# Operands of the matmuls placed by their byte distance modulo 256, and two AdaLN norms of the second block folded into the feed-forward that follows

## The reference, cut to what matters

```
h = modulate(rmsnorm_2(x, ffn1_norm[l]), sh1, sc1)          # norm(x) * gain * (1 + sc) + sh
x = x + 0.5 * (1 + g1) * swiglu_2(h, ffn1_w_gate[l], ffn1_w_up[l], ffn1_w_down[l])
h = modulate(rmsnorm_2(x, mix_norm[l]), sh2, sc2)
x = x + (1 + g2) * hybrid_mixer(h, ...)
h = modulate(rmsnorm_2(x, ffn2_norm[l]), sh3, sc3)
x = x + 0.5 * (1 + g3) * swiglu_2(h, ...)
return rmsnorm_2(x, final_norm)
```

## Time and profile before

| what | value |
|---|---|
| median of three runs | 2888.78 us |
| profiled execution | 2889.2 us |
| its span on the core | 2887.4 us |
| granted TensorE clock, mean | 0.982 |
| TensorE matmul busy | 2785.5 us (96%), 17408 matmuls |
| VectorE busy | 1905.4 us (66%) |
| ScalarE busy | 1200.3 us (42%) |
| GpSimd busy | 608.2 us (21%) |
| chain that ended last | TensorE 71%, VectorE 14%, issue 6%, ScalarE 4% |
| VectorE subtraction for `in_lo`, 128x2048 (336), mean | 2.40 us; 2.29 us where GpSimd is idle |
| VectorE product of 128x256 (1316, 1321) | 0.42 us |
| VectorE four splits of features (615) | 1.65 us |
| VectorE squaring 128x1024 (716) | 1.22 us |
| VectorE, two diagonals (2076) | 0.48 us |
| GpSimd, 1/rms of two columns (839, 840) | 0.19 and 0.69 us |
| a ReLU unit | 11.15 us |

### The profile page before, as it was taken

One profiled execution on the slowest core, in us unless ns is written; L12 is line 12 of the kernel. 1 busy time (PEld: TensorE's weight loads), 2 busy tenths in 40 slices (PEclk: granted clock), 3 DMA queues, 4 the chain that ended last, 5 costly groups with the idle time before them and its releaser, 6 DMA issues.

```text
span 2887.4 us, 43862 instructions
## 1 busy us (share of the span) xinstructions
PE 2785.5 (96%) x17408; PEld 2457.0 (85%) x17408; DVE 1905.4 (66%) x2046; ACT 1200.3 (42%) x1478; POOL 608.2 (21%) x510
## 2 busy tenths in 40 slices
PE   8999999999989989999899999999999989999998
PEld 8987789989878988998699898888788878888887
DVE  7885655688867885555655556666666747665665
ACT  4333444333444334334444345334433444445433
POOL 5953200068435851000100000000000320000000
PEclk9999999999999999999899999999999999999999
DMA  7755135557526764433345444545554335533542
GB/s 289 258 182 162 45 146 192 187 210 270 188 74 227 264 229 176 185 142 103 110 180 191 144 133 182 201 148 168 194 198 154 120 138 200 199 128 114 211 189 102
DMA packets 126465, 500.31 MB, mean 173 GB/s; under 512 B 11024, under 2 KB 12336, under 8 KB 92960
## 3 DMA queue, kind: packets, MB, share of 16 engines
q1 hardware_dynamic: 112768, 450.39, 42.9%
q0 software_dynamic: 13600, 48.60, 4.9%
HBM read 497.90 MB, written 1.05 MB: 173 GB/s over the span
## 4 chain that ended last, share of the span: by engine, by line
PE 71%; DVE 14%; issue 6%; ACT 4%; DMA 2%; POOL 2%; DVEq 0%; SPq 0%; ACTq 0%; POOLq 0%
PE duo L1105 7%; PE duo L1198 6%; PE duo L1202 6%; PE duo L1206 6%; PE duo L1107 5%; PE duo L1108 5%; PE duo L1115 5%; DVE down_lo L336 4%; PE duo L1114 4%; PE duo L1500 3%; PE duo L1501 3%; PE duo L1505 3%; DVE in_lo L336 3%; DVE hid_hi L1326 2%; ACT in_hi L329 2%
## 5 line engine op out<-in xcount | busy, mean ns | idle before, releaser
L336 DVE TENSOR_TENSOR in_lo<-ring_in,in_hi 128x2048 fp32r<-128x2048 f32 x296 | 709.9, 2399 | 304.7 <-ACT in_hi L329 304.5
L329 ACT CAST in_hi<-ring_in 128x2048 fp32r<-128x2048 f32 (+1 forms) x293 | 554.7, 1893 | 274.0 <-PE duo L1505 136.0
L336 DVE TENSOR_TENSOR down_lo<-ring_down,down_hi 128x1024 fp32r<-128x1024 f32 (+1 forms) x196 | 372.1, 1898 | 33.6 <-ACT down_hi L329 33.6
L1107 PE MATMUL duo<-feat,in_hi 128*128 128x256 f32 x1408 | 344.9, 284 | 4.0 <-ACT in_hi L329 3.4
L1108 PE MATMUL duo<-feat,in_hi 128*128 128x256 f32 x1408 | 343.9, 283 | 0.0
L329 ACT CAST down_hi<-ring_down 128x1024 fp32r<-128x1024 f32 (+1 forms) x196 | 260.2, 1327 | 71.4 <-PE duo L1206 70.1
L1107 PEld LDWEIGHTS duo<-feat,in_hi 128*128 128x128 f32 x1408 | 270.0, 192 | 8.7 <-ACT in_hi L329 3.8
L1108 PEld LDWEIGHTS duo<-feat,in_hi 128*128 128x128 f32 x1408 | 270.4, 192 | 3.3
L1198 PE MATMUL duo<-down_hi,hid_hi 128*128 128x512 f32 x984 | 260.0, 396 | 7.5 <-DVE hid_hi L1326 6.6
L1202 PE MATMUL duo<-down_lo,hid_hi 128*128 128x512 f32 x984 | 259.8, 396 | 0.0
L1206 PE MATMUL duo<-down_hi,hid_lo 128*128 128x512 f32 x984 | 258.7, 394 | 0.0
(11 more groups left out here) (493 smaller groups left out, 5147.5 us busy)
## 6 DMA issues: line engine op xcount, KB each, us to landing
ring_in<-in_ffn_in SPq DMA_DIRECT2D x196, 1024.0 KB, 6.2
ring_down<-in_ffn_down SPq DMA_DIRECT2D x132, 512.0 KB, 3.5
ring_down<-in_ffn_down SPq DMA_DIRECT2D x64, 1024.0 KB, 4.8
mod_w<-in_w_ada POOLq DMA_DIRECT2D x72, 512.0 KB, 5.0
ring_in<-in_sb_w_qkv SPq DMA_DIRECT2D x24, 1024.0 KB, 5.2
ring_in<-in_conv_w_in SPq DMA_DIRECT2D x12, 1024.0 KB, 5.1
ring_in<-in_gla_w_in SPq DMA_DIRECT2D x12, 1024.0 KB, 5.1
ring_in<-in_nsa_w_in SPq DMA_DIRECT2D x10, 1024.0 KB, 5.2
```

The lines of the kernel that those rows point to most:

```text
L329: act.copy(hi[:, s, 0:n], raw[:, s, 0:n]).then_inc(hi_ready.sem, 1)
L336: dve.tensor_tensor(lo[:, s, 0:n], raw[:, s, 0:n], hi[:, s, 0:n].bitcast(F32), ALU.subtract).then_inc(lo_ready.sem, 1)
L1107: pe.matmul(out, hi, self.feat_hi[:, c, :], start=opens, stop=False, skip_group_check=True)
```

## The change

Three things are done.

First, placement. `feat` gets 2 x 8 rows of 288 elements (1152 bytes) of space. Unnamed gap tiles put `in_hi` 64 bytes past the start of `feat_space` modulo 256, and `proj` and `arena` 64 bytes before `in_hi`, so that `hid_*` and `down_*` have difference 0. Two views of 256-column rows start at byte 0 of the space (`feat_near`, difference 64 to `in_hi`) and byte 64 (`feat`, difference 0). `Feed` with `for_silu` or `moves`, `RowFeed` and `FeatTurn` use `feat_near`; the others keep `feat`, and `Feed` after a `Linear` keeps `feat2`, whose difference to `in_hi` stays 64.

Second, `ShiftRowFeed` replaces `row_norm` and `pre_norm` ahead of `ffn1_in_2`, and `ShiftFeed` replaces `pre_norm` ahead of `ffn2_in_2`. They are `RowFeed` and `Feed` with the AdaLN scale as gain. `HybridOut` now transposes the first half of x between the two halves of its last unit.

Third, the offset `sh` rides along as two more feature columns: each row of features is 258 columns wide (`WIDE_FEATURE`), at a row distance of 1152 bytes, so that rows with even c have a difference of 64 to the weights and rows with odd c one of 192. Gate and up products take a PSUM bank each; VectorE copies the two columns that the offset gives (`shifts`), multiplies gate and up by 1/rms, and ScalarE adds the gate's offset inside SiLU. The pre-norm ahead of `HybridIn` stays.

```diff
-        self.feat = split("feat", 2, KC, TOKENS)
-        self.feat_hi, self.feat_lo = self.feat[:, 0], self.feat[:, 1]
+        self.feat_space = split("feat", 2 * KC * WIDE_ROW)
+        near, still = (self.feat_space[:, at:at + 2 * KC * TOKENS].rearrange("p (s c n) -> p s c n", s=2, c=KC) for at in (0, NEAR // 4))
+        self.feat_wide = self.feat_space[:, :].rearrange("p (s c n) -> p s c n", s=2, c=KC)[:, :, :, 0:WIDE_FEATURE]
+        self.feat, self.feat_near = still, near
+        self.feat_hi, self.feat_lo = self.feat[:, 0], self.feat[:, 1]
+        phase("in_gap", nc.sbuf_base - 4 * 2 * KC * WIDE_ROW + NEAR)
+        at_in = nc.sbuf_base
...
+        phase("hidden_gap", at_in - NEAR)
...
+        phase("arena_gap", at_in - NEAR)
...
         act.wait_ge(k.turned.sem, self.t0 + c + 1)
-        act.activation(self.feat_hi[:, c, :], self.home(c), ACT.Copy, scale=k.col(self.gain, c)).then_inc(k.turn_hi.sem, 1)
+        if c == 0 and self.shift is not None:
+            act.copy(self.feat_hi[:, :, TOKENS:], self.shift)
+        act.activation(self.feat_hi[:, c, 0:TOKENS], self.home(c), ACT.Copy, scale=self.gain_of(c)).then_inc(k.turn_hi.sem, 1)
...
+                    if self.shifted:
+                        self.gate.tensor(pe)
...
+    def _multiply_shifted(self, dve, m, j):
+        k = self.k
+        pair, whole, up, shifts = k.duo[2 + j], k.act[:, j, 0:TOKENS], k.act[:, j, TOKENS:2 * TOKENS], self._shifts(j)
+        if isinstance(m, int) and m + j == 0:
+            self._diagonals(dve)
+            dve.wait_ge(k.rrow_ready.sem, self.rr0 + 1)
+        dve.wait_ge(k.in_used.sem, m + (self.u0 + j + 1))
+        dve.tensor_copy(shifts, pair[:, :, TOKENS])
+        dve.tensor_tensor(whole, pair[:, 0, 0:TOKENS], self.rrow, ALU.mult).then_inc(k.gate_scaled.sem, 1)
+        dve.tensor_tensor(up, pair[:, 1, 0:TOKENS], self.rrow, ALU.mult).then_inc(k.up_scaled.sem, 1)
+        dve.wait_ge(k.act_ready.sem, m + (self.ac0 + j + 1))
+        dve.wait_ge(k.up_scaled.sem, m + (self.us0 + j + 1))
+        dve.scalar_tensor_tensor(whole, up, shifts[:, 1:2], whole, ALU.add, ALU.mult).then_inc(k.raw_ready.sem, 1)
+        self._hand_over(dve, m, j, whole, k.hid_hi[:, j, 0:TOKENS])
+        if isinstance(m, int) and m + j == 0:
+            self.feeds.first_multiplied(dve)
...
             if i == 3 and t == 1:
+                self.follow.turn(pe, 0)
                 pe.wait_ge(self.mean, self.mean0 + 1)
...
     def scalar(self, act):
-        for i in range(2, 6):
+        for i in range(2, 5):
             in_hi(self.k, act, self.u0 + i)
+        for c in range(self.early_hi):
+            self.follow.hi(act, c)
...
         in_lo(k, dve, self.u0 + 4)
+        for c in range(self.early_lo):
+            self.follow.lo(dve, c)
         self._with_row(dve, 0, 1, False)
         self._with_row(dve, 1, 1, False)
-        in_lo(k, dve, self.u0 + 5)
...
-    plan.extend(row_norm(k, plan[-1], "final_norm", row))
-    weights = MlstmWeights(k, plan[-1])
-    gate = [GateRow(k, mod, 0, (6, 7)), GateRow(k, mod, 1, (0, 1)), GateRow(k, mod, 2, (6, 7))]
-    plan.extend(pre_norm(k, plan[-1], mod.scale(0), mod.shift(0)))
-    plan.insert(-1, weights)
-    plan.append(FeedForward(k, plan[-1], "ffn1_in_2", "ffn1_down_2", True, "row", [], gate=gate[0]))
+    feed = ShiftRowFeed(k, plan[-1], mod, 0, "final_norm", row)
+    weights = MlstmWeights(k, feed)
+    gate = [GateRow(k, mod, 0, (2, 3)), GateRow(k, mod, 1, (0, 1)), GateRow(k, mod, 2, (2, 3))]
+    plan.extend([feed, weights])
+    plan.append(FeedForward(k, feed, "ffn1_in_2", "ffn1_down_2", True, "row", [], gate=gate[0]))
...
-    plan.extend(pre_norm(k, plan[-1], mod.scale(2), mod.shift(2)))
+    plan.append(ShiftFeed(k, plan[-1], mod, 2))
...
-        feed = Feed(k, plan[-1], gain, True) if i else RowFeed(k, plan[-1], gain, "final_norm_2", k.mod_w[:, 0, :])
+        feed = Feed(k, plan[-1], gain, True, moves=i in (2, 3)) if i else RowFeed(k, plan[-1], gain, "final_norm_2", k.mod_w[:, 0, :])
```

More of the change, by code:

```diff
@@ L542, with __init__ @@
 class Feed(Stage):
-    def __init__(self, core, before, gain, after_ffn, for_silu=False, for_relu=False):
+    def __init__(self, core, before, gain, after_ffn, for_silu=False, for_relu=False, moves=False):
         super().__init__(core, before)
         self.gain, self.after_ffn, self.for_silu, self.for_relu = gain, after_ffn, for_silu, for_relu
+        self.shift = None
         self.value = core.x
@@ L671, in __init__ @@
     def __init__(self, core, before, gain, row, home):
-        super().__init__(core, before, gain, True)
+        super().__init__(core, before, gain, True, moves=True)
         self.row, self.row_home = ROW_VECTORS.index(row), home
         self.value = core.y
+        self.unread_act = [core.proj[:, t, 0:D] for t in range(TT)]
+        self.unread_dve = [core.proj[:, t, D:2 * D] for t in range(TT)]
         before.row_feed = self
@@ L737, in gpsimd, with __init__, _modulated, gain_of @@
         pool.tensor_tensor(k.stat("factor"), k.stat("acc_mean"), half, ALU.pow).then_inc(k.factor_ready.sem, 1)
+class ShiftFeed(Feed):
+    def __init__(self, core, before, mod, branch):
+        super().__init__(core, before, None, False)
+        self._modulated(mod, branch, core.feat2_wide)
+    def _modulated(self, mod, branch, wide):
+        self.mod, self.branch = mod, branch
+        self.feat_hi, self.feat_lo = wide[:, 0], wide[:, 1]
+        self.shift = mod.columns[:, 3 * branch, :].unsqueeze(2).broadcast_to([P, KC, 2])
+    def gain_of(self, c):
+        return self.mod.scale(self.branch)(c)
+    def first_multiplied(self, dve):
+        pass
+class ShiftRowFeed(ShiftFeed, RowFeed):
+    def __init__(self, core, before, mod, branch, row, home):
+        RowFeed.__init__(self, core, before, None, row, home)
+        self._modulated(mod, branch, core.feat_wide)
+        self.unread_act = [core.mod_w[:, 0, :], core.arena[:, 13952:13952 + D]]
+        self.unread_dve = [core.mod_w[:, 1, :], core.act[:, :, :].rearrange("p a n -> p (a n)")]
+    def squares_act(self, act):
+        act.wait_ge(self.mod.summed.sem, 3)
+        super().squares_act(act)
+    def squares_dve(self, dve):
+        dve.wait_ge(self.mod.summed.sem, 3)
+        super().squares_dve(dve)
+    def settle(self, dve):
+        pass
+    def first_multiplied(self, dve):
+        RowFeed.settle(self, dve)
 class FeatTurn(Stage):
@@ L1117, in _opens @@
     def _opens(self, h, c):
-        return c == 0 and (h == 0 or not self.silu)
+        return c == 0 and (h == 0 or self.shifted or not self.silu)
     def _hidden(self, pe, m, j):
@@ L1153, in _first_hidden @@
                     last = self._low(pe, 0, h, c)
-                if q == 0 and h == 0 and not isinstance(self.feeds.feeds, Load):
+                if q == 0 and h == int(self.shifted) and not isinstance(self.feeds.feeds, Load):
                     self.feeds.turn(pe, 1)
@@ L1179, in _spread_rstd @@
         for t in range(TT):
-            last = pe.matmul(k.bank[6][:, t * P:(t + 1) * P], k.c("ones", 0, P), self.diagonal[:, t, :], start=True, stop=True)
+            last = pe.matmul(k.bank[self.spread_bank][:, t * P:(t + 1) * P], k.c("ones", 0, P), self.diagonal[:, t, :], start=True, stop=True)
         last.then_inc(k.rrow_spread.sem, 1)
@@ L1238, in tensor @@
             self._first_two(pe)
-        if self.gate:
+        if self.gate and not self.shifted:
             self.gate.tensor(pe)
```

75 lines of the change are left out of this document (58 added, 17 removed).

## The result

The kernel after takes 2869.64 us (median of six runs, 2863.02 to 2874.36) against 2888.93 for the kernel before in the same rounds (six runs, 2882.9 to 2894.02): ratio 0.9934, 95% interval 0.9919 to 0.9949. It is faster by 19.3 us, 0.66%; the forecast was 38.9 us, 2850, with 2872 as the upper end of its range. The direction held, but only half of the gain came.

A forecast was written before the change was run, and what follows sets the result against it. TensorE was taken as the bound, its feed-forward time being the number of matmuls times their pitch. Terms a to f, 8 + 2 + 6.6 + 7 + 9.2 + 6.1 = 38.9 us, took 2889.2 to 2850, range 2826 to 2872.

The forecast's parts named there:

- e: Edge ahead of `ffn1_in_2`: first down matmul at 1097.5 instead of 1106.75, saving 9.2 us; bounds 5 and 12.
- f: Edge ahead of `ffn2_in_2`: gate row and 36 matmuls done at 1449.8 against 1455.89, saving 6.1 us; bounds 3 and 9.
- c: `ffn1_in_2` and `ffn2_in_2`, distance 0 to 64 and 192 by turns, 258 columns: 0.15 us per unit, 6.6 us saved.
- a: Down matmuls of the feed-forwards, distance 128 to 0, get a faster pitch: 8 us saved; range 3 to 18.
- a, ReLU: Down matmuls in 64 ReLU units, distance 128 to 0: 0.1 us saved per unit, 6.4 us.
- a, SiLU: Down matmuls in 66 SiLU units of three stages without `ModPart`, distance 128 to 0: 0.025 us per unit, 1.6 us saved.
- b: `ffn1_in0` and `ffn1_in1`, distance 0 to 64: 2 us saved for both, as TensorE waits for VectorE; bounds -3 and 12.3.
- d: Projections that move features in `QkvIn`, `GlaIn` and `HybridIn`, 1344 matmuls at a faster pitch: 7 us saved; bounds 2 and 8.
- rival 4: Waits for 1/rms grow, or the clock falls to 1.2 GHz in them; both edges give 5, not 15.3: 2860; chance 0.14.
- Rival 1: Placement does nothing; only the two edges' gains stay and the wide rows cost 1.8 us: 2876; chance 0.10.

The follow-up runs named there:

- e1: Kernel after with the SiLU feed-forwards' hidden activations 128 bytes further on, so their down matmuls are at distance 128 again: 2869.67 us, ratio 0.9938.
- m1: Separate kernel, TensorE alone repeating a unit's matmuls on zeros at chosen distances; hidden at 64: 8.40 us with down at 0, 8.24 to 8.25 with down at 128.
- m3: Separate TensorE-only kernel for the wide rows; rows 1152 bytes apart, down at 0: unit 8.500 us with 258 columns, 8.367 with 256.
- e6: e1 with GpSimd's multiplications and additions in `ModPart` cut from 1024 to 8 columns, loads kept: 2846.39 us, one run.
- e7: e5 with the hidden activations of the SiLU feed-forwards that are not wide 192 bytes further on (down at distance 192): 2853.27 us, ratio 0.9889.
- e10: e7 with the gate row ahead of the whole second unit, ReLU features at distance 192, down and wide rows moved by 64 bytes: 2853.26 us, ratio 0.9886.
- e5: Kernel after with the gate row's four matmuls ahead of TensorE's wait for 1/rms instead of behind it: 2858.86 us, ratio 0.9905.
- e3: Placement alone: kernel after with the second block's norms and edges as in the kernel before, 256 columns there at distance 64: 2870.14 us, ratio 0.9936.

## Why the prediction was right in direction and wrong in size

The letters are the terms of the prediction's sum. Three steps failed: in e and f the clock behind the new waits, in c the price of two columns, and in a the reading of the pitch as a thing of one instruction.

- *a, ReLU*: right in size and reason. 11.153 to 11.053 us a unit, 5.6 us between the first and last down matmuls of the four stages (6.4 forecast for all 64 units).
- *a, SiLU*: **the failed step in the mechanism**. The prediction had a SiLU unit save "2 x 5.8 = 0.01 us" by counting only the down matmuls that run fast. It treated the pitch as a property of one instruction and its two addresses. Down at distance 0 put the 48 matmuls behind it at 117.6 instead of 113.3 ns: +0.153 us a unit, 3.1 us lost in `ffn2_in0`, where a gain of 0.5 was forecast. The earlier trace rows showed a pitch at distance 64 *with down at 128*, and that condition was not read as one; e1 and m1 show it. The ten matmuls at the slower pitch in the earlier trace rows can be read as a hint that the sequence matters.
- *c*: **a failed term**, 1.3 us instead of 6.6. The two extra columns were priced at 0.8 ns. They cost 2.4 to 7.5 ns a matmul (117.6 or 113.3 to 120.0 or 120.8, m3), and the turning of the distances kept the pitch from 113 as well. The measured gain lies nearer to the lower bound, -1.8, than to what was taken.
- *b*: the reason was right (VectorE held by GpSimd, e6), the size too hopeful: `ffn1_in0` and `ffn1_in1` took 0.7 us more where 2 us less were forecast, `ffn2_in1` 1.6 us more where 0 stood. Behind it stands a misread row. The earlier trace rows name the same two stops twice, once for the weight load and once for the matmul, so their 4.8 and 4.4 us must not be added. TensorE was idle for 4.4 us there (170.00 less 165.58, in the window of the kernel before), and in `ffn1_in0` for 0.8 and not 1.8 us. What did show the limit are the lengths before, 171.8 us at distance 0 and 172.3 at 64. With base units of 8.53 and 8.25 (before), 8.40 (after) and 8.25 us (e1) the three took 516, 519 and 518 us. The bound of -3 held. The rule that a faster TensorE only gets to wait for VectorE held in the kernel after and in e1; in e7 to e10 the three took 511 to 518 us, which differs from run to run too much to tell.
- *d*: right. Lines 2164 to 2166 (2033 to 2035 before) at 113.4 ns between waits instead of 120; 1344 matmuls gave 2.5 + 2.6 (`QkvIn`), 0.7 (`GlaIn`) and 2.2 us (`HybridIn`), 8.0 in all for 7.
- *e and f*: **the failed step that cost most**. 3.6 and 0.9 us instead of 9.2 and 6.1, a miss of 10.8 us (f from the transposes at 1425.50 to 1452.19, 26.7 us, against 27.6 for the same work before). The waits were right; the gate row, "only moved", was priced at 1.98 us and took 3.4 and 3.7, and the 36 matmuls behind it 6.1 and 6.8 us instead of 4.3, since the clock was at 0.50. Together that is 3.3 and 4.2 us. Of the other 3.3 us, 1.2 are the first unit of `ffn1_in_2`, which started later than drawn up; the rest was not taken apart. This is the second half of rival 4, which had a chance of 0.14 and a time of 2860, with 5 us for e and f together (measured 4.5). In e5 the edges shrank by 11.6 us: about 6 of those 7.5 us (at the second edge the 36 matmuls still took 5.9), 1.9 at each edge because the gate row now stands inside the wait, and a rest that was not taken apart. The prediction had seen the half clock in the earlier trace rows and had put it down to the long gap alone.
- Not forecast: the mixers and ends outside d, e and f, 8.4 us shorter, less the 3.0 us of clock in the first mixer. Most of it is there with the placement alone (e3: 475.2 us in the three mixers, 328.5 in the rest). Which of the placements did it was not tried, and part of it differs from run to run.

Sum: the forecast of 38.9, less 10.8 (e and f), 5.3 (c), 2.7 (b), 1.6 (`ffn2_in1`, for which 0 stood), 4.7 (a, SiLU: 1.6 forecast, -3.1 measured in `ffn2_in0`, the wide stages being under c) and 0.8 (a, ReLU), plus 1.0 (d), is 14.0. The span fell by 19.5; the remaining 5.5 are the last point's. Without them the time would have been outside the range of 2826 to 2872, so that it lies inside is in part luck. Rival 1 (placement does nothing, from the Trainium skill, TensorE: Matmul & The Clock Gate, "Part 2: What happens when you issue a matmul") would have come close to the time, 2876, and was wrong: with nothing else running, a unit lasts from 8.187 to 8.533 us by the addresses alone, with 256 columns in all of them.

## What to carry to other kernels

Where TensorE is the bound, measure the repeated sequence of matmuls alone, for each placement you can choose, before you move an operand; a pitch read off one instruction's row held here only with the same neighbours. Price a matmul of another width from a row of its own: two more columns cost three to nine times their share here. And when a step is moved to stand behind a new wait, price it at half the clock, or let it fill the wait, as e5 did.
